# Combine stage of a two-block layer: the next tile's transposes ahead of the last projection chunk, and the second tile's sum among the weight splits

## The reference

```
h  = h + sum over the 4 chosen experts of gates[k] * y_rows[k]     # end of moe
gate = sigmoid(rms_norm(h, norm_ple_w) @ ple_gate_w)               # 1024 x 1024
h  = h + gate * (p @ ple_proj_w)                                   # 256 x 1024
x2 = rms_norm(h, final_norm_w)                                     # output of block 1
z  = rms_norm(x2, pre_norm_g_2) @ w_in_2                           # 1024 x 1984
```

## Time and profile before

| what | value |
|---|---|
| median of 3 runs | 5829.93 us (5826.6 to 5834.68) |
| the profiled execution | 5826.38 us, span 5824.6 us |
| mean granted TensorE clock over the span | 0.962 |
| TensorE busy over the span | 5316.9 us (91%) |
| the combine stage in the span | from about 3684 to 4436 us |

### The profile page before, as it was taken

The page is one execution under the profiler, slowest core; times in us unless marked ns, Lnnn a source line. Parts: engine busy times, 40 slices in busy tenths (PEclk is TensorE's granted clock), DMA queues, the critical chain, the costliest instruction groups (busy, mean ns, idle before and its releaser), DMA issues. The chain is left out here.

```text
span 5824.6 us, 77622 instructions
## 1 busy us (share of the span) xinstructions
PE 5316.9 (91%) x24587; PEld 3508.7 (60%) x24922; DVE 3248.5 (56%) x6128; ACT 2129.4 (37%) x3190; POOL 707.8 (12%) x901
## 2 busy tenths in 40 slices
PE   6999999499999999999999999599995599999688
PEld 3555555366666666666666666355554477777365
DVE  3433433477676767777777777433335544443277
ACT  3111111144443545555555554222222433333243
POOL 0000000100000000000000000001003399100000
PEclk9999999699999999999999999799997799999899
DMA  3111211356464647777777676422322300000433
GB/s 136 57 50 54 72 50 50 115 176 192 159 207 150 211 152 238 237 237 240 239 232 234 229 227 204 161 93 103 103 89 97 82 5 8 6 6 6 170 108 101
DMA packets 424599, 769.80 MB, mean 132 GB/s; under 512 B 57440, under 2 KB 142368, under 8 KB 422816
## 3 DMA queue, kind: packets, MB, share of 16 engines
q1 hardware_dynamic: 363984, 607.16, 31.5%
q10 hardware_dynamic: 33216, 87.05, 4.9%
q0 software_dynamic: 27280, 74.02, 4.0%
HBM read 628.36 MB, written 139.76 MB: 132 GB/s over the span
## 5 line engine op out<-in xcount | busy, mean ns | idle before, releaser
L1070 DVE TENSOR_TENSOR w_lo<-stage,w_hi 128x1024 bf16<-128x1024 f32 (+1 forms) x800 | 929.6, 1178 | 201.3 <-ACT w_hi L939 142.3
L939 ACT ACTIVATE w_hi<-stage 128x1024 fp32r<-128x1024 f32 (+1 forms) x800 | 791.7, 1017 | 575.9 <-PE GU L773 291.2
L770 PE MATMUL GU<-w_hi,x_hl 128*128 128x512 f32 x2048 | 860.1, 420 | 19.0 <-DVE x_hl L1075 7.6
L771 PE MATMUL GU<-w_hi,x_hl 128*128 128x512 f32 x2048 | 811.6, 396 | 0.0
L636 PE MATMUL PJ<-w_in_sb,xT 128*128 128x512 f32 x1280 | 579.6, 607 | 41.9 <-ACT w_in_sb L376 31.5
L773 PE MATMUL GU<-w_lo,x_bf 128*128 128x512 bf16 x1920 | 480.6, 381 | 7.7
L770 PEld LDWEIGHTS GU<-w_hi,x_hl 128*128 128x128 f32 x2048 | 386.5, 189 | 135.1 <-issue 27.9
L770 PE MATMUL Y<-w_hi,a_hl 128*128 128x512 f32 x1024 | 456.8, 446 | 0.0
L636 PEld LDWEIGHTS PJ<-w_in_sb,xT 128*128 128x128 f32 x1280 | 244.2, 195 | 332.8 <-issue 286.2
L771 PEld LDWEIGHTS GU<-w_hi,x_hl 128*128 128x128 f32 x2048 | 387.5, 189 | 82.9
L771 PE MATMUL Y<-w_hi,a_hl 128*128 128x512 f32 x1024 | 404.4, 395 | 0.0
(11 more groups left out here) (537 smaller groups left out, 8752.2 us busy)
## 6 DMA issues: line engine op xcount, KB each, us to landing
stage<-in_expert_w_gate_up_dram SPq DMA_DIRECT2D x512, 512.0 KB, 5.2
stage<-in_expert_w_down_dram SPq DMA_DIRECT2D x224, 512.0 KB, 6.7
expert_rows<-zero_y SPq DMA_DIRECT2D x16, 2048.0 KB, 10.0
b_gu<-in_expert_b_gate_up_dram ACTq DMA_DIRECT2D x128, 256.0 KB, 4.9
expert_rows<-acted ACTq DMA_DIRECT2D x64, 512.0 KB, 2.9
b_d<-in_expert_b_down_dram ACTq DMA_DIRECT2D x32, 512.0 KB, 8.0
stage<-in_expert_w_down_dram SPq DMA_DIRECT2D x64, 256.0 KB, 3.3
z<-z_sb SPq DMA_DIRECT2D x16, 992.0 KB, 8.1
```

The lines of the kernel that those rows point to most:

```text
L770: pe.matmul(out, high(k), w_high(k), start=(k == first), stop=False)
L771: pe.matmul(out, low(k), w_high(k), start=False, stop=False)
L939: act.activation(w_hi[:, c, ks, :], staged, ACT.Copy).then_inc(s["hi_done"], 1)
L1070: dve.tensor_tensor(w_lo[:, c, ks, :], staged, w_hi[:, c, ks, :], ALU.subtract).then_inc(s["lo_done"], 1)
```

## The change

Three queues are reordered; no arithmetic is changed.

- TensorE: inside a step, the transposes of the *next* tile (`turn`, `turn_p`) stand ahead of the last of the four projection chunks, no longer after it. At the start, small product 0, the transposes of `h` 1 and gate product 1 come before the first projection in a new order: `turn(0), turn_p(0), gate(0), small_product(0), turn(1), gate(1), turn_p(1)`, then the steps. Inside, `turn(t + 1)` waits for `h2_done >= t + 2`, the signal behind the sum of tile `t + 1`, and `turn_p(t + 1)` for `h3_done >= t + 1`.
- ACT: `square_h` of the next tile comes after the second `copy_z`, the copies of `hT` and `pT` after the third. At the start, ACT's `gate(0)`, `square_h(1)` and `copy_hT(1)` stand after the fourth of eight high parts, `square_3(0)` and `square_2(0)` after the sixth.
- DVE: `combine` is cut into `add_rows` and `scale_of`. At the start, `add_rows(1)` stands ahead of the low parts and `finish(0)` after the sixth of them.

```diff
@@ scalar queue, a step
+                    copy_z(t - 1, 1 - par, 1, has_prev)
+                    if has_next:
+                        square_h(t + 1, 1 - par)
+                    copy_z(t - 1, 1 - par, 2, has_prev)
+                    if has_next:
+                        copy_hT(t + 1)
+                        copy_pT(t + 1)
+                    copy_z(t - 1, 1 - par, 3, has_prev)
@@ scalar queue, start
-            body(0, 0, True, False)
-            body(1, 1, True, False)
+            square_h(0, 0)
+            copy_hT(0)
+            copy_pT(0)
+            act.wait_ge(s["gains"], 48)
+            high_weights(range(4))
+            gate(0)
+            square_h(1, 1)
+            copy_hT(1)
+            high_weights((4, 5))
+            square_3(0, 0)
+            square_2(0, 0)
+            high_weights((6, 7))
+            copy_pT(1)
+            body(1, 1, True, True, False)
@@ vector queue, start
             combine(0, 0)
...
-            for k in range(KD):
-                dve.wait_ge(s["proj_hi"], k + 1)
-                dve.scalar_tensor_tensor(w_lo[:, k, :], z_sb[:, k % 2, :], gain_pre[:, k:k + 1], w_hi[:, k, :],
-            for t in (0, 1):
-                if t == 1:
-                    low_x2(0)
-                finish(t, t, False)
-                combine(t + 1, 1 - t)
+            add_rows(1, 1)
+            low_weights(range(6))
+            finish(0, 0, False)
+            low_weights((6, 7))
+            scale_of(1)
+            low_x2(0)
+            finish(1, 1, False)
+            combine(2, 0)
@@ tensor queue, a step
+            def body(t, par, has_prev, has_this, has_next):
+                if has_this and not is_step(t, 1):
+                    gate(t)
+                pe.wait_ge(s["x2_done"], t)
...
+                if has_this:
+                    small_product(t)
+                pe.wait_ge(s["x2T_sb"], t * 3)
+                if is_step(t, 1):
+                    pe.wait_ge(s["proj_lo"], KD)
+                for n, (lo, hi) in enumerate(Z_CHUNKS):
+                    if n == len(Z_CHUNKS) - 1 and has_next:
+                        turn(t + 1, 1 - par)
+                        turn_p(t + 1, 1 - par)
...
+            turn(0, 0)
+            turn_p(0, 0)
+            gate(0)
+            small_product(0)
+            turn(1, 1)
+            gate(1)
+            turn_p(1, 1)
+            body(1, 1, False, True, True)
```

More of the change, by code:

```diff
@@ L1430, in copy_hT, with copy_pT @@
                 act.activation(hT[:, 4:8, :], TR[:, BANK:], ACT.Copy).then_inc(s["hT_sb"], 1)
+            def copy_pT(t):
                 act.wait_ge(s["pT_ps"], t + 1)
@@ L1464, in copy_z, with high_weights @@
                                scale=rstd_2[:, par:par + 1]).then_inc(s["z_sb"], 1)
-            def high_weights():
-                act.wait_ge(s["gains"], 48)
-                for k in range(KD):
+            def high_weights(ks):
+                for k in ks:
                     act.wait_ge(s[f"proj_in{k % 2}"], 16 * (k // 2 + 1))
@@ L1471, in high_weights, with body @@
                                    scale=gain_pre[:, k:k + 1]).then_inc(s["proj_hi"], 1)
[L1473 to L1479, removed]
+            def body(t, par, has_this, has_next, has_prev):
                 if not is_step(t, 0):
                     copy_x2T(t - 1)
-                if has_next:
+                if has_this:
                     gate(t)
@@ L1486, in body @@
                     copy_z(t - 1, 1 - par, 0, has_prev)
-                if has_next:
+                if has_this:
                     square_2(t, par)
                 if not is_step(t, 0):
-                    for n in range(1, len(Z_CHUNKS)):
-                        copy_z(t - 1, 1 - par, n, has_prev)
-            body(0, 0, True, False)
-            body(1, 1, True, False)
-            body(2, 0, True, False)
+                    copy_z(t - 1, 1 - par, 1, has_prev)
[20 more added lines that the diff above has]
+            body(1, 1, True, True, False)
+            body(2, 0, True, True, False)
             with act.Fori(1, TILES // 2 - 1) as i:
[L1497 to L1500, removed]
+                body(i * 2 + 1, 1, True, True, True)
+                body(i * 2 + 2, 0, True, True, True)
+            body(TILES - 1, 1, True, False, True)
+            body(TILES, 0, False, False, True)
         @block.vector
@@ L1511, in low_x2, with add_rows @@
                                       x2_hi[:, 4 * n:4 * n + 4, :], ALU.subtract).then_inc(s["x2T_sb"], 1)
-            def combine(t, par):
+            def add_rows(t, par):
                 dve.wait_ge(s["y_in"], t * (16 * TOPK) + 16 * TOPK)
@@ L1524, in combine, with scale_of @@
                 dve.sem_inc(s["h2_done"], 1)
+            def scale_of(t):
                 dve.wait_ge(s["sumsq_h"], t + 1)
@@ L1543, in finish, with combine, low_weights @@
                 inv_rms(dve, ch, rstd_2[:, par:par + 1], ss_2[:, :], nt[:, :], D, EPS, s["rstd_2_ready"])
+            def combine(t, par):
+                add_rows(t, par)
+                scale_of(t)
+            def low_weights(ks):
+                for k in ks:
+                    dve.wait_ge(s["proj_hi"], k + 1)
+                    dve.scalar_tensor_tensor(w_lo[:, k, :], z_sb[:, k % 2, :], gain_pre[:, k:k + 1], w_hi[:, k, :],
+                                             ALU.mult, ALU.subtract).then_inc(s["proj_lo"], 1)
             combine(0, 0)
@@ L1549, in _ @@
                 dve.tensor_scalar(w_gate[:, k, :], w_gate[:, k, :], gain_ple[:, k:k + 1], None, ALU.mult).then_inc(s["gate_scaled"], 1)
-            for k in range(KD):
-                dve.wait_ge(s["proj_hi"], k + 1)
-                dve.scalar_tensor_tensor(w_lo[:, k, :], z_sb[:, k % 2, :], gain_pre[:, k:k + 1], w_hi[:, k, :],
-                                         ALU.mult, ALU.subtract).then_inc(s["proj_lo"], 1)
-            base, first = ch.n, True
-            for t in (0, 1):
-                if t == 1:
-                    low_x2(0)
-                finish(t, t, False)
-                combine(t + 1, 1 - t)
+            add_rows(1, 1)
[3 more added lines that the diff above has]
+            scale_of(1)
+            base = ch.n
+            low_x2(0)
+            finish(1, 1, False)
+            combine(2, 0)
+            per = (ch.n - base) * 2
             with dve.Fori(1, TILES // 2 - 1) as i:
-                per = (ch.n - base)
-                ch.start(i * per + base)
+                ch.start(i * per + (base - per // 2))
                 for u in range(2):
@@ L1567, in _ @@
                 assert ch.n == per, ch.n
-            ch.start(base + per * (TILES // 2 - 1))
+            ch.start(base + per // 2 + per * (TILES // 2 - 2))
             low_x2(TILES - 3)
@@ L1578, in _ @@
             pe.wait_ge(s["ident_ready"], 1)
[L1580 to L1584, removed]
-                    for k in range(KD):
[L1586 to L1589, removed]
-                    for k in range(PLE // P):
[L1591 to L1633, removed]
+            def turn(t, par):
+                pe.wait_ge(s["h2_done"], t + 1)
+                for k in range(KD):
+                    mm = pe.transpose(TR[:, k * P:(k + 1) * P], h[:, par, k * P:(k + 1) * P], ident[:, :])
+                mm.then_inc(s["hT_ps"], 1)
@@ new lines, in turn_p, with gate @@
+            def turn_p(t, par):
+                if not is_step(t, 0):
+                    pe.wait_ge(s["h3_done"], t)
+                for k in range(PLE // P):
+                    mm = pe.transpose(PP[:, k * P:(k + 1) * P], p_sb[:, par, k * P:(k + 1) * P], ident[:, :])
+                mm.then_inc(s["pT_ps"], 1)
+            def gate(t):
+                pe.wait_ge(s["hT_sb"], t + 1)
+                if is_step(t, 0):
+                    pe.wait_ge(s["gate_scaled"], KD)
+                else:
+                    pe.wait_ge(s["tanh_done"], t)
+                for n in range(2):
+                    for k in range(KD):
+                        mm = pe.matmul(G[:, n * BANK:(n + 1) * BANK], hT[:, k, :], w_gate[:, k, n * BANK:(n + 1) * BANK],
+                                       start=(k == 0), stop=(k == KD - 1))
+                mm.then_inc(s["g_ps"], 1)
@@ new lines, in small_product @@
+            def small_product(t):
+                pe.wait_ge(s["pT_sb"], t + 1)
+                if is_step(t, 0):
+                    pe.wait_ge(s["ple_in"], 16 * (PLE // P))
+                for n in range(2):
+                    for k in range(PLE // P):
+                        mm = pe.matmul(PP[:, n * BANK:(n + 1) * BANK], pT[:, k, :], w_ple[:, k, n * BANK:(n + 1) * BANK],
+                                       start=(k == 0), stop=(k == PLE // P - 1))
+                mm.then_inc(s["pp_ps"], 1)
@@ new lines, in body @@
+            def body(t, par, has_prev, has_this, has_next):
+                if has_this and not is_step(t, 1):
+                    gate(t)
+                pe.wait_ge(s["x2_done"], t)
+                for k in range(KD):
```

(18 more changed lines are left out.)

## The result

The changed kernel has a median of 5787.56 us (5780.96 to 5791.17, 4 runs) against 5829.75 us of before. The ratio is 0.9924, 95% interval [0.9912, 0.9937]. That is 42.2 us less, where 30.8 were forecast; the ratio applied to the median of before gives 5785, just under the forecast's lower end of 5787, while the median itself, 5787.56, is just above it. A later repeat of both on one chip gave 5791.53 against 5828.13 us, ratio 0.9943 [0.9929, 0.9956], 36.6 us less. So the gain is some 37 to 42 us, and 30.8 was too little.

What follows compares the result with a forecast made beforehand. TensorE was taken to bound the steps, where only gaps can be won, but not the start, where it waits for DVE's sum; 18.6 - 1.5 + 13.7 = 30.8 us off 5829.9 gives 5799, 8 in 10 range 5787 to 5812.

Steps and rivals of the forecast that it cites:

- the clock: TensorE at half clock after idling in the new start: a loss between 0 and 3 us, taken as 1.5.
- the step: Each step in DVE's loop: gap of 1.81 us removed, new wait of 0.92 added, net 0.89 us, 12 times.
- later stages start behind a barrier and keep their lengths: Stages after the combine stage: no change in their time was forecast.
- The start: Up to the first projection matmul: reordered queues bring it from 3796.9 to 3778.3, a gain of 18.6 us.
- The upper bound of 22.3: Gain at the start if tile 2's fetches did not share with the loads; loads 3 to 5 come 3.8 us earlier.
- The gap of 1.81 us: Ahead of G in each step, start to start: said to go with the copies under the last chunk.
- the new wait: TensorE's wait on `h2_done` ahead of each step's last chunk: a new gap of 0.92 us.
- The one step outside DVE's loop: Tile 15, whose sum takes 5.25 us: gap about 0.6 us, net gain 1.2 us.
- the wait eats the steps: Rival, in the steps: DVE's sum ends 1 us later, leaving 17.1 us of gain, 5813 us; 13 in 100.
- the wait vanishes: Rival, in the steps: no new wait, so they give 25.3 us, total 42.4, 5788 us; 8 in 100.
- the start gives half: Rival, at the start: slower loads 2 to 5 and the clock leave 9 us, not 17; 5807 us; 12 in 100.
- the slower case: Rival, in the steps: TensorE waits on a late fetch or load, 3.0 us more per step, 5842 us; 3 in 100.

Runs made afterwards that it cites:

- the chain 4.2 us shorter: The change with transposes inside the last chunk, tile 2's fetch held back, and tile 1's scale and ACT's copy of pT earlier: 5775.66 us, ratio 0.9907.
- the extra operation: The kernel before with one more DVE operation of 1.28 us at the end of each finish, result unused: 5828.04 us, ratio 0.9998.
- the last run: The kernel before, unaltered, profiled a second time: 5829.42 us, ratio 0.9999.
- the steps alone: The change with the start of TensorE, ACT and DVE put back to the order before, against the kernel before: 5807.88 us, ratio 0.9963.
- the padded run: The change with one more DVE operation of 1.28 us in each finish, ahead of the next tile's sum: 5825.06 us, ratio 0.9995.

## Why the prediction fell short

The mechanism was right in the stage: both parts gave what they were said to give, for the reasons worked out. The stage gave 35.5 us for 30.8, since two terms were mis-sized: the clock (1.5 us put down, 0 measured) and the step (0.89 us put down, 1.10 measured). These alone would give a time of 5794 us, well inside the range. The step that failed, and that carried the result to the range's edge, is a third one, "later stages start behind a barrier and keep their lengths". In the first pair of profiles another 4.7 us and 2.7 us more in the medians came from outside the stage. The repeat shows little of that: 36.6 us in the medians, with the same 35.5 in the stage.

**The start: right, 18.8 for 18.6.** The chain that the forecast worked through is the one in the trace: the sum of tile 1 waits for its rows (6.83 us idle ahead of it), then low parts, the fifth and sixth late behind their loads, `finish(0)`, low 6 and 7, the scale, `low_x2`. The pieces differ from the forecast and happen to cancel. Loads 2 and 3 were put at 6.6 and 8.4 us, loads 4 and 5 at 5.0; the trace has 4.8, 6.6, 6.6 and 6.8. So the closeness of 18.6 to 18.8 is in part luck. One reason is that the fetch started later than I assumed: its first DMA was issued by 3738.7, where POOL's usual lengths (0.18 + 0.83 + 0.96 us from 3733.51) give 3735.5. The other is that load 3 queues behind load 2. The share was different too: from 3741 to 3744 the weight queue moved 0.57 MB and the fetch's 0.56, where the forecast had taken 61% from the earlier trace rows. The upper bound of 22.3 was also slightly off: by the same chain undisturbed loads end it 3.5 us earlier and not 3.8. POOL's timeline:

```profile
3733.51 2.26 POOL L1405 COPY slots<-pos 128x4 int32 x1 [15.56 <-DVEq L1537]
3736.59 2.15 POOL L1408 DMA_INDIRECT y_rows<-expert_rows,slots  x1 [0.83 <-POOL slots L1405]
3739.05 0.94 POOL L1408 DMA_INDIRECT y_rows<-expert_rows,slots  x1 [0.31 <-issue]
```

A copy that usually takes 0.18 us took 2.26, and the first fetch 2.15 in place of 0.96. DVE's low parts 0 and 1 ran from 3733.44 to 3737.92, and POOL's copy ends where the first of them does. The Trainium skill, "SBUF — State Buffer", section "SBUF: two separate sides", says that GpSimd and DVE share a pair of ports as a lock, that a DVE instruction with two SBUF inputs takes it against a GpSimd instruction that reads SBUF, and that whichever starts second is blocked for the whole of the other's instruction. The rows fit that for the copy: where the fetch is held back behind six low parts, the same copy took 0.19 us. For the slow fetch no run here isolated a cause; in the held-back run it took 1.59 us.

**The clock: 0 where 1.5 was put down.** "Between 0 and 3 I take 1.5". The lower clock came, but over the small product alone (6.21 us for 3.60). That ended at 3778.57, just before DVE's `low_x2` (3778.66), which the first chunk waits for anyway; the first projection matmul followed at 1.00, and the term was 0. In the repeat the small product ended 0.96 us before its first chunk. The windows of TensorE (length, busy, granted clock, DMA share, GB/s) show where the clock fell, in the middle of the gap ahead of the small product:

```profile
3768.30:3770.50 2.20, 0.03 (x1) 1.00 0.47 188
3770.90:3772.30 1.40, 0.00 (x0) 0.50 0.91 287
3772.40:3777.00 4.60, 4.60 (x6) 0.50 0.12 43
```

The experiments show how near it was: with the chain 4.2 us shorter the same fall cost the first chunk 1.5 us.

**The steps: right in kind, 1.10 a step where 0.89 was worked out.** The gap of 1.81 and the new wait are both there. I had costed the pieces between the wait and the next step at their lengths of before: transposes to chunk 1.09, chunk 4.97, G 13.84. They now follow one another in another order and take 1.07, 4.86 (3878.46 to 3883.32) and 13.74. Twelve times 0.2 is 2.4 us. The one step outside DVE's loop gave 1.4, forecast 1.2, and gate product 2 came 2.1 earlier, forecast 1.8.

**What is beyond the stage: "later stages keep their lengths".** In the first pair of profiles they gave 4.7 us, and that pair's medians are 2.7 apart beyond the profiles. Together with the terms above this is the miss: 1.5 + 2.4 + about 0.8 in the stage, 4.7 and 2.7 outside it, less 0.6 ahead of it.

Is the change the cause of the 4.7? For more than half of it, no. ACT's first copy `outs` comes some 262 to 265 us after the next stage's first POOL instruction (4443.41 before, 4443.57 before with the extra operation, 4408.44 with the change, 4410.11 in its repeat). In this order:

```profile
4708.04 0.60 ACT L2236 ACTIVATE outs<-O 128x512 f32<-128x512 f32 x1 [1.61 <-PE O L2473]
4705.67 0.60 ACT L2237 ACTIVATE outs<-O 128x512 f32<-128x512 f32 x1 [1.61 <-PE O L2474]
4670.56 0.60 ACT L2281 ACTIVATE outs<-O 128x512 f32<-128x512 f32 x1 [1.61 <-PE O L2518]
4674.77 0.60 ACT L2281 ACTIVATE outs<-O 128x512 f32<-128x512 f32 x1 [1.60 <-PE O L2518]
```

That is 264.63, 262.10, 262.12 and 264.66 us. So 2.5 of the 4.7 us arise in this stretch. The unaltered repeat of the change doesn't save them, and the old order with the extra operation saves them in full: this code takes either of two lengths, with both orders. Whether the change makes the short one more frequent isn't settled: the long one came in 2 of 3 profiles with the old order (264.94 in the last run) and in 1 of 10 with either or both parts changed. Behind this point the two groups overlap (1114.8 to 1118.4 us and 1114.2 to 1117.9). Over the whole rest the three have 1381.2, 1379.8 and 1380.5 us, the ten 1376.3 to 1380.75, with a mean 2.7 us lower. What precedes the stage varied by 10 us (3686.6 to 3696.8) over all profiles with no change in it. What chooses between the two lengths stays open.

**The rivals.** That the wait eats the steps fell with the first run of the steps alone. That the wait vanishes is false for the change and true for the version with the transposes inside the chunk. That the start gives half fell with the 18.8 us. No run came near the slower case, but the padded run shows that too much delay was allowed for it. I had the sign turn at 2.2 us more per step. The stage did lose 2.2 us per step, but the delay that did it was only 1.33 us: the lower clock did the rest, and 4.2 us of the stage's 35.5 were left.

## What to carry to other kernels

When a wait for a second engine is moved ahead of work that doesn't need it, look at where in that work the signal really arrives, and put the waiting instructions there: here 1.8 us later was worth 9.4 us in all and left TensorE no wait for DVE. With the wait in place, each microsecond added on DVE cost one or more in every step; how much DVE can grow behind the later place before it costs again, no run tried. Cost a gap on TensorE twice, once for its length and once for the clock it may bring down with it, and don't take that from the gap's length alone: 1.91 us brought it down in some steps, and 2.69 us did not in another start. And for a whole program, compare a stage's length inside its own marks: here the spans and medians moved by 3 to 7 us for reasons outside the edited stage.

## What the hardware showed unexpectedly

- TensorE's clock fell after idle gaps of 1.91 us in seven of twelve otherwise equal steps, 0.1 to 1.2 us after work had resumed at 1.00, and after one of 3.72 us about one microsecond into the work. In the change itself it fell within the gap of 4.03 us, and the small product began at 0.50. With gaps of 0.59 and 1.37 us it stayed at 1.00 in all steps, with 1.64 us too, and with 2.69 and 2.65 us in the start with the fetch held back.
- POOL's copy and first fetch took 2.26 and 2.15 us beside DVE's 128x1984 operation with two f32 inputs, and 0.18 and 0.96 in the later steps.
- A matmul sequence took about 0.1 us less per change of neighbour: the last chunk 4.86 after 4.97 us, G 13.74 after 13.84.
